# Small pieces woven two to a slot instead of one, in a three-branch layer kernel

## Time and profile before

| | |
|---|---|
| time, median of 3 runs | 1643.45 us |
| profiled execution, first to last instruction | 1642.1 us |
| TensorE matmul, busy | 1632.2 us (99%), 7776 matmuls |
| TensorE weight load, busy | 1352.8 us (82%) |
| VectorE, busy | 934.3 us (57%) |
| ScalarE, busy | 775.9 us (47%) |
| weights' DMA, busy share of 16 engines | 57.0% |

### The profile page before, as it was taken

How to read it: one execution, slowest core, us unless ns; L and a number is a source line. 1 busy time by engine, 2 the same in 40 slices (tenths; PEclk the granted TensorE clock), 3 DMA queues, 4 the chain that set the end, 5 groups by cost and what they waited for, 6 DMA issues and landing times.

```text
span 1642.1 us, 19738 instructions
## 1 busy us (share of the span) xinstructions
PE 1632.2 (99%) x7776; PEld 1352.8 (82%) x7776; DVE 934.3 (57%) x1388; ACT 775.9 (47%) x1062; POOL 24.6 (1%) x51
## 2 busy tenths in 40 slices
PE   8999999999999999999999999999999999999999
PEld 6888888888888888888878888888888888888887
DVE  5655555657545454544769565564445666665554
ACT  6644444495343343433555455454445444444332
POOL 3000000000000000000000000000000100000000
PEclk9999999999999999999999999999999999999999
DMA  8655666756545455554555455456665755566674
GB/s 283 190 180 182 205 188 193 189 149 191 153 138 167 142 162 145 149 159 142 168 155 185 160 182 164 155 185 192 189 192 167 255 169 179 168 191 190 193 239 161
DMA packets 163337, 293.15 MB, mean 179 GB/s; under 512 B 22170, under 2 KB 26924, under 8 KB 163244
## 3 DMA queue, kind: packets, MB, share of 16 engines
q1 hardware_dynamic: 161084, 284.02, 57.0%
q0 software_dynamic: 2160, 7.87, 1.4%
HBM read 287.65 MB, written 4.19 MB: 178 GB/s over the span
## 4 chain that ended last, share of the span: by engine, by line
PE 98%; DVE 1%; ACT 0%; DMA 0%; issue 0%; SPq 0%
PE acc L535 30%; PE acc L537 29%; PE acc L536 29%; PE mix L634 3%; PE mix L508 3%; PE mix L756 1%; PE mix L616 0%; PE mix L737 0%; DVE w_lo L1197 0%; PE mix L592 0%; PE mix L775 0%; DMA w_raw<-in_w_in_dram 0%; ACT w_hi L868 0%; PE mix L734 0%; PE mix L719 0%; PE mix L717 0%
## 5 line engine op out<-in xcount | busy, mean ns | idle before, releaser
L1197 DVE TENSOR_TENSOR w_lo<-w_raw,w_hi 128x1024 fp32r<-128x1024 f32 (+1 forms) x536 | 645.8, 1216 | 463.6 <-ACT w_hi L868 462.0
L535 PE MATMUL acc<-w_hi,op_hi 128*128 128x512 f32 (+1 forms) x2048 | 819.9, 400 | 0.9 <-DVE w_lo L1197 0.9
L537 PE MATMUL acc<-w_hi,op_lo 128*128 128x512 f32 (+1 forms) x2048 | 801.0, 391 | 0.0
L536 PE MATMUL acc<-w_lo,op_hi 128*128 128x512 f32 (+1 forms) x2048 | 798.3, 390 | 0.0
L868 ACT ACTIVATE w_hi<-w_raw 128x1024 fp32r<-128x1024 f32 (+1 forms) x536 | 557.2, 1050 | 450.4 <-PE acc L537 441.7
L537 PEld LDWEIGHTS acc<-w_hi,op_lo 128*128 128x128 f32 x2048 | 384.9, 188 | 83.6
L535 PEld LDWEIGHTS acc<-w_hi,op_hi 128*128 128x128 f32 x2048 | 385.5, 188 | 78.4 <-DVE w_lo L1197 2.7
L536 PEld LDWEIGHTS acc<-w_lo,op_hi 128*128 128x128 f32 x2048 | 385.9, 188 | 74.9
L1329 DVE SCALAR_TENSOR_TENSOR cT<-mix,par,cT 128x255 f32<-128x255 f32 (+2 forms) x72 | 29.1, 475 | 18.1 <-ACT cT L958 18.1
L1097 ACT ACTIVATE b_p<-b_s,st 128x128 f32<-128x128 f32 (+1 forms) x32 | 14.3, 446 | 49.4 <-DVE st L1522 49.4
L994 ACT ACTIVATE c_gam<-mix 128x256 f32<-128x256 f32 x24 | 9.2, 385 | 59.9 <-PE mix L508 59.9
(11 more groups left out here) (277 smaller groups left out, 822.0 us busy)
## 6 DMA issues: line engine op xcount, KB each, us to landing
w_raw<-in_w_in_dram SPq DMA_DIRECT2D x368, 512.0 KB, 3.8
w_raw<-in_w_out_dram SPq DMA_DIRECT2D x128, 512.0 KB, 3.8
w_raw<-in_w_in_dram SPq DMA_DIRECT2D x16, 384.0 KB, 3.3
w_raw<-in_a_wuq_dram SPq DMA_DIRECT2D x12, 512.0 KB, 4.5
xs<-in_x_dram SPq DMA_DIRECT2D x7, 512.0 KB, 5.7
w_raw<-in_a_wuqi_dram SPq DMA_DIRECT2D x6, 512.0 KB, 3.6
y<-in_x_dram POOLq DMA_DIRECT2D x6, 512.0 KB, 8.4
out_dram<-y POOLq DMA_DIRECT2D x5, 512.0 KB, 3.7
```

What stands on the lines that cost most here:

```text
L535: nc.tensor.matmul(o, hi[:, kt, tok], hv[:, i, :], start=(kt == blk["kts"][0]), stop=False)
L536: nc.tensor.matmul(o, hi[:, kt, tok], lv[:, i, :], start=False, stop=False)
L537: last_mm = nc.tensor.matmul(o, lo[:, kt, tok], hv[:, i, :], start=False, stop=(kt == blk["kts"][-1]))
L1197: vec.tensor_tensor(split_ap(w_lo, c), w_raw[:, c % RAW_BUFS, 0:n], split_ap(w_hi, c).bitcast(F32), ALU.subtract).then_inc(lo_ready, 1)
```

## The change

In `plan()` two neighbouring pieces of the same or of adjacent steps are put into one slot as a list: the two `conv` of a block, two steps of `csq` and `cn`, `cv` with `ck` or `cs`, `bt` in pairs, `bsc` in pairs, `bo` of one part with `bs` of the next, `ap` of one head with `ae` of the next, and `yt` in pairs. In TensorE's loop `x_columns` is called twice after every even chunk instead of once after each. No instruction is added or removed; every engine issues the same instructions, some in another order and slot. There are fifty groups of small matmuls fewer: 7 of x, 6 `conv`, 4 `cn`, 4 `cv`, 2 `bt`, 4 `bsc`, 8 `bo`, 7 `ap`, 8 `yt`.

One thing follows from how `weave` returns its next slot. The last `conv` pair stands in slot 97 and the next free slot is 103, where it was 109 before. So the gates' steps and all of branch C begin six slots earlier, and `bn` stands in slot 239, where it was 245; from `bit` (slot 260) on the steps stand where they stood, up to a slot or two within a head.

```
     for j in range(6):
-        at = weave(end("conv", j) + 2, [("conv", 2 * j), ("conv", 2 * j + 1)], 6)
-    for i in range(10):
-        at = weave(at, [([("csq", i)] if i < 8 else []) + ([("cn", i - 2)] if i > 1 else [])])
+        at = weave(end("conv", j) + 2, [[("conv", 2 * j), ("conv", 2 * j + 1)]], 6)
+    for i in range(0, 10, 2):
+        at = weave(at, [[piece for k in (i, i + 1) for piece in
+                         ([("csq", k)] if k < 8 else []) + ([("cn", k - 2)] if k > 1 else [])]], 2)
...
-        at = weave(at, [("cv", u), ("ck", u) if m == 0 else ("cs", u), ("cr", u), ("co", u), ("cy", u), None])
+        at = weave(at, [[("cv", u), ("ck", u) if m == 0 else ("cs", u)], None, ("cr", u), ("co", u), ("cy", u), None])
     at = max(at, end("bkv", 512) + 1)
-    at = weave(at, [("bn", 0), None, None, ("bkn", 0), None, None] + [("bt", i) for i in range(4)] + [("bkt", 0)])
+    at = weave(at, [("bn", 0), None, None, ("bkn", 0), None, None] + [[("bt", 0), ("bt", 1)], None, [("bt", 2), ("bt", 3)], None,
+                                                                          ("bkt", 0)])
...
-    at = weave(end("bi", 0) + 1, [("bit", 0)] + [("bsc", (0, p)) for p in range(4)])
-    at = weave(max(at, end("bi", 1) + 1), [("bit", 1)] + [("bsc", (1, p)) for p in range(4)])
+    for j in range(2):
+        at = weave(max(at, end("bi", j) + 1), [("bit", j), [("bsc", (j, 0)), ("bsc", (j, 1))], None,
+                                               [("bsc", (j, 2)), ("bsc", (j, 3))], None])
...
         for v in range(3):
-            at = weave(at, [("bs", (g, v)), None, ("bp", (g, v)), ("bo", (g, v))])
+            at = weave(at, [[("bo", (g, v - 1)), ("bs", (g, v))] if v else ("bs", (g, v)), None, ("bp", (g, v))])
+        at = weave(at, [("bo", (g, 2))])
...
-    weave(first + 4, [("yt", i) for i in range(4, 16)])
+    weave(first + 5, [[("yt", i), ("yt", i + 1)] for i in range(4, 16, 2)], 2)
     at = end("av", 1) + 2
     for h in range(H_A):
-        at = weave(at, [("ae", h), None, None, ("ap", h), None, None, ("ay", h), None])
-    at = weave(at + 1, [("yt", i) for i in range(4)], 2)
+        at = weave(at, [[("ap", h - 1), ("ae", h)] if h else ("ae", h), None, None, None,
+                        [("ay", h - 1)] if h else None, None, None])
+    at = weave(at, [("ap", H_A - 1), None, None, ("ay", H_A - 1), None])
+    at = weave(at + 1, [[("yt", i), ("yt", i + 1)] for i in range(0, 4, 2)], 3)
...
-                if c + X_AHEAD < NX:
+                if c % 2 == 0 and c + X_AHEAD < NX:
                     x_columns(c + X_AHEAD)
+                    x_columns(c + X_AHEAD + 1)
```

## The result

The changed kernel takes 1651.42 us, the median of four runs (1650.83 to 1652.06), against 1643.49 for the kernel before on the same chip: ratio 1.0049, interval [1.0037, 1.0061]. It is 7.9 us slower; 1649.9 was forecast, in a range of 1645 to 1654.5. Its profiled execution has a span of 1649.5 us, 7.4 above the one of before.

What follows compares the result with a forecast made beforehand. TensorE, 98% of the chain, was taken to bound the kernel, with the helpers hidden behind it. Stalls 10.5 plus `bn` 0.1 minus joins 4.1 gave +6.5 on 1643.45: 1649.9 us, range 1645 to 1654.5.

Steps and rivals of the forecast that it cites:

- The stalls at `conv`: Six joined `conv` pairs delay a later split, so TensorE waits 1.91 us once and 1.71 five times: 10.5 us.
- `conv` joins as savings: Joining the transposes of the six `conv` pairs saves TensorE 0.07 us each.
- The 23 joins of transposes: Joining 7 pairs of x, 6 `conv`, 2 `bt` and 8 `yt` saves TensorE 0.07 us each, 1.6 us.
- `bsc`, 1.2 us: Four joins of `bsc` groups with 64-row matmuls save TensorE 0.3 us each, between 0.07 and 0.5.
- `cn`, nothing: Four joins of `cn` matmuls with ones save nothing, having no price beyond their own work.
- The 19 unlike joins: Joining 4 `cv`, 8 `bo` with `bs`, 7 `ap` with `ae` saves 0.07 us each, taken from transposes: 1.3 us.
- `bn` in slot 239: `bn` now shares its slot with block 14's silu; the helpers' chain there costs 0 to 0.2 us, taken as 0.1.
- rival 2: More stalls in the moved part, one to three places at 1.3 us: 1651.2 to 1653.8 us; chance 0.08.
- The other joins cost the helpers nothing: Outside `conv`, joins add less helper work than the margins before the splits, so they cost nothing.
- Rival 1: The joins work and `conv` doesn't stall: 1639.4 us; chance 0.10.
- Rival 3: The clock falls after each of the six stalls, losing 2.2 us each: 1662.9 us; chance 0.04.
- Rival 4: The joins save TensorE nothing, small matmuls just costing what they cost: 1654.1 us; chance 0.03.

Runs made afterwards that it cites:

- e2: The kernel before with only the two `conv` of a block joined in one slot, all later pieces in their old slots: 1654.23 us.
- e1: The changed kernel with the two `conv` of a block back in slots six apart, all other joins kept: 1640.65 us.
- e4: The changed kernel, `conv` still joined, with ScalarE's wait for VectorE and both silus moved three slots later: 1640.62 us.
- e8: The kernel before with x, `bt`, `cv`, `bsc`, `bo`, `yt` joined, `conv` joined with silus three slots later, `csq`, `cn`, `ap`, `ae` single: 1640.05 us.
- e3_conv_adjacent: The changed kernel with the second `conv` of a block one slot behind the first instead of in the same slot: 1643.61 us.

## Why the prediction was right, and where its terms were off

- *The stalls at `conv`, 10.5 us.* Measured 10.4 in the changed kernel, at the six chunks named. The steps of the sum held: 3.88 us for one more `conv` (116.68 - 112.80), 0.45 instead of 0.42 for TensorE's larger group (3.87 - 3.42), and the margin of 1.75 leave 1.68, against 1.71 measured. The first pair was forecast at 1.91 and waited 1.73; in e2, where x is not joined, it waited 1.89. e2 and e1 show that nothing else of the change is needed for the waits, e4 that it is the wait ahead of silu.
- *What a wait leaves behind* was missing from the sum: 0.13 us in the chunk behind each of the six, and 0.17 behind the one at chunk 243, 0.9 in all.
- *`conv` joins as savings, 6 x 0.07.* A joined group costs 115.74 - 111.87 - 2.95 = 0.92 against 0.47 and 0.49 for the two single ones, so 0.04; e8, where nothing waits, has 0.3 us for the six, 0.05 each.
- *The 23 joins of transposes, 1.6 us*: the 17 outside `conv` gave 1.24, the 6 of `conv` 0.3. *`bsc`, 1.2 us*: 1.3. That term was the middle of wide bounds, and that it came so near is in part luck: of the 0.33 a join, 0.13 is what follows a group, which the sum didn't have. *`cn`, nothing*: nothing. *The 19 unlike joins, 1.3 us*: 0.56. This was the term taken from a row of another kind of group, and it was mis-sized: `cv` gave what transposes give, `bo` half of it, `ap` with `ae` lost a little. All joins together gave 3.4 us, added up by class, instead of 4.1. (The prediction's lower bound for them adds up to 1.4 us, not 1.5.)
- *`bn` in slot 239, 0.1 us.* A wait of 0.19 at chunk 243, (0.42 us from 785.46 to 785.88 instead of 0.23), within the 0 to 0.2. No other new wait of a chunk appeared in the moved part, and rival 2 fell.
- *The other joins cost the helpers nothing.* True of the changed kernel; But `csq` and `cn` had been cleared too lightly. The prediction read margins of 5 to 8 us for them; in the trace before, the splits behind slots 111 to 115 were ready only 2.7 to 4.5 us ahead. And a margin of the split says nothing of a piece whose matmuls need a square made in an earlier slot: that is where e1 waits, at a cost of 0.4 us, with these pieces in their old place. In the changed kernel they stand six slots earlier and nothing waits.
- *The rivals.* Rival 1 (no stall) is what e1 and e4 make of the kernel, and there it came true, at 1640.6 us against the 1639.4 of the rival. Rival 3 (the clock) fell: pauses of 1.7 us left the granted clock at full, and from the second step on the matmuls behind them at 0.23 us from start to start. The section "A second HAM failure mode: psum-queue depth-cycling" of the Trainium skill's "TensorE: Matmul & The Clock Gate" had suggested it might fall; with six such pauses some 46 us apart no run here shows it. Rival 4 (the joins save nothing) fell with e1, 2.6 us below the kernel before, and the table above.

In sum: 10.4 + 0.2 + 0.9 - 3.4 = 8.1 us, against 7.9 timed and 6.5 forecast: the mechanism was right, and the two terms that were off, what a wait leaves behind and the joins, were off the same way. By the traces it is 8.4 us (7.96 from chunk 1 on, and the 0.44 of x), so some 0.3 is not accounted for. The spans differ by 7.4 because the opening of the profiled execution, but for that 0.44, happened to be 1.0 us shorter.

## What to carry to other kernels

Before work is put together in one slot, look for a wait between two engines inside the piece. There the pieces add up whole, the wait included. What has to be compared with their sum is not an engine's busy share (ScalarE's was 47%) but the time until the next thing behind it is due. That margin can be read in the trace before anything is built; here it predicted five of the six stalls to 0.1 us and the first to 0.2. When such a wait is the trouble, move the wait and what depends on it to a later slot and leave the rest joined.

## What the runs showed of the hardware

- A chunk behind a break of TensorE's stream of main matmuls takes longer. Behind the plain wait before chunk 37, and behind four float32 transposes, it is 2.85 us instead of 2.72; behind the wait in e3_conv_adjacent 2.86. Most of it is the first step, 0.33 us from the first matmul to the second (122.89 to 123.22) where 0.227 is usual; the next five to nine mostly start 0.23 to 0.236 us apart. Behind the `cn` groups the long first step does not appear (328.61 to 328.84 before). Why was not settled.
- For transposes, what a join saves is this and no more. Eight in one group take 0.08 us more between main matmuls than two groups of four (0.80 against 2 x 0.36), and 0.13 is saved behind. With the 64-row matmuls of `bsc` the join itself saves another 0.20.
- The opening, up to chunk 1, differed by 1.5 us between profiled executions with the same opening code (12.66 and 14.20 us; with x joined 13.63 and 15.12), more than most of the effects looked for here.
